# Gating and adding two expert rows on ScalarE and GpSimd, and part of the ALPHA x addition on VectorE

## What is computed

```python
# end of layer 0: combine the experts, post-norm
y = y + dense_gate[:, e:e + 1] * (h @ w_down[e])      # two experts per token have a gate
x = layer_norm(ALPHA * x + f, ln_ffn_g[0], ln_ffn_b[0])
# layer 1: causal pooling over trailing windows 2/4/8/16, one per group of 256 channels
pooled = means - x
mixed = einsum('btgc,gcd->btgd', pooled, w_pool) * pool_scale
x = layer_norm(ALPHA * x + mixed, ln_mix_g[1], ln_mix_b[1])
# then the router of layer 1 reads x
logits = x @ w_router
```

## Time and profile before

| | us |
|---|---|
| median of three runs | 1658.82 (1653.52 to 1663.27) |
| the profiled execution | 1659.36 |
| its span, first to last instruction | 1657.6 |
| mean granted TensorE clock | 0.927 of full |
| busy: TensorE, VectorE, ScalarE, GpSimd | 1457.2, 635.0, 365.4, 205.5 |
| the stage `combine_pool_mix` | about 1134 to 1272 |

### The profile page before, as it was taken

The page is one execution under the profiler, slowest core; times in us unless marked ns, Lnnn a source line. Parts: engine busy times, 40 slices in busy tenths (PEclk is TensorE's granted clock), DMA queues, the critical chain, the costliest instruction groups (busy, mean ns, idle before and its releaser), DMA issues. The chain is left out here.

```text
span 1657.6 us, 27544 instructions
## 1 busy us (share of the span) xinstructions
PE 1457.2 (88%) x10747; PEld 890.2 (54%) x10748; DVE 635.0 (38%) x1062; ACT 365.4 (22%) x788; POOL 205.5 (12%) x263
## 2 busy tenths in 40 slices
PE   6999999957778898999929999994996599999968
PEld 4566666645578886444414444442795344444423
DVE  1122453079245452776461111114795311111127
ACT  1233110066423332111101111111232011111111
POOL 4000000000133322110001101104000110110040
PEclk9999999987789999999959999996697699999989
DMA  6573110041110002110259788785105778786453
GB/s 189 134 290 121 26 26 26 0 113 27 30 26 4 5 4 71 56 39 26 111 169 314 267 303 289 254 282 181 62 1 186 269 246 314 257 281 227 159 209 124
DMA packets 137060, 236.96 MB, mean 143 GB/s; under 512 B 20178, under 2 KB 100115, under 8 KB 136682
## 3 DMA queue, kind: packets, MB, share of 16 engines
q1 hardware_dynamic: 113458, 151.01, 28.7%
q0 software_dynamic: 16880, 60.41, 9.9%
q10 hardware_dynamic: 6624, 24.12, 3.6%
HBM read 178.84 MB, written 58.21 MB: 143 GB/s over the span
## 5 line engine op out<-in xcount | busy, mean ns | idle before, releaser
L2257 PE MATMUL ex_pb<-ew_w_gate_up,ex_xT 128*128 x736 | 329.8, 601 | 6.0 <-DVE ex_xT L2302 2.3
L298 PE MATMUL pj_pb<-pj_xT,pj_w 128*128 128x348 f32 (+3 forms) x960 | 282.1, 455 | 0.8 <-ACT pj_xT L322 0.8
L298 PEld LDWEIGHTS pj_pb<-pj_xT,pj_w 128*128 128x128 f32 (+1 forms) x960 | 178.8, 186 | 101.9 <-ACT pj_xT L322 0.8
L2257 PEld LDWEIGHTS ex_pb<-ew_w_gate_up,ex_xT 128*128 128x128 f32 x736 | 138.0, 193 | 165.0 <-issue 164.0
L2240 PE MATMUL ex_pb<-ew_w_down,ex_hiddenT 128*128 x368 | 165.7, 593 | 3.4 <-ACT ex_hiddenT L2327 3.4
L2450 DVE TENSOR_TENSOR ex_hidden<-ex_hidden,ex_pb 128x256 f32<-128x256 f32 x46 | 19.4, 421 | 324.4 <-ACT ex_hidden L2322 324.4
L2240 PEld LDWEIGHTS ex_pb<-ew_w_down,ex_hiddenT 128*128 128x128 f32 x368 | 66.3, 190 | 69.9 <-issue 69.9
L2445 DVE COPY ex_y_rows<-ex_pb 128x512 f32<-128x512 f32 x46 | 31.8, 692 | 134.5 <-PE ex_pb L2240 134.5
L430 DVE SCALAR_TENSOR_TENSOR mixed<-pj_pb,v_mu,mixed 128x347 f32<-128x347 f32 (+3 forms) x42 | 24.0, 572 | 145.7 <-ACT mixed L372 145.6
L2322 ACT ACTIVATE ex_hidden<-ex_pb 128x256 f32<-128x256 f32 x46 | 17.7, 384 | 261.3 <-PE ex_pb L2257 261.3
L1888 PE MATMUL mo_pb<-late_rows,projected_qkv 128*128 128x512 f32 (+1 forms) x144 | 66.6, 608 | 0.0
(11 more groups left out here) (414 smaller groups left out, 2031.4 us busy)
## 6 DMA issues: line engine op xcount, KB each, us to landing
ew_w_gate_up<-in_w_ex_gate SPq DMA_DIRECT2D x32, 1024.0 KB, 8.2
ew_w_gate_up<-in_w_ex_up SPq DMA_DIRECT2D x32, 1024.0 KB, 10.9
ew_w_down<-in_w_ex_down SPq DMA_DIRECT2D x32, 1024.0 KB, 12.9
scratch_slots_out<-ex_y_rows ACTq DMA_DIRECT2D x46, 512.0 KB, 4.8
scratch_slots_out<-pj_tmp POOLq DMA_DIRECT2D x4, 4096.0 KB, 16.7
scratch_x_stored<-x_rows SPq DMA_DIRECT2D x16, 512.0 KB
pj_w<-in_w_in SPq DMA_DIRECT2D x7, 1024.0 KB, 8.9
minus_kk_then_y<-in_x_prompt SPq DMA_DIRECT2D x8, 512.0 KB, 6.0
```

The source lines that it names most:

```text
L298: last = nc.tensor.matmul(product(at)[:, 0:tn], w[:, s % NW, k, c0:c0 + mrows], xT[:, k, x0:x0 + tn], start=(k == 0), stop=(k == KD - 1))
L2257: last = mm(pb[:, 2 + u, :], xT[:, u, k, :], w[:, k, :], start=(k == 0), stop=(k == KD - 1))
```

## The change

ScalarE multiplies both gathered rows by their gates, in place. GpSimd adds row 1 to row 0, and VectorE adds ALPHA x to that sum in one instruction. GpSimd issues the gathers of the first three tiles, then for each tile the add and the gather of the tile three further on. In the pooling products, TensorE's diagonal adds ALPHA x for the first two groups (columns 0 to 511) only; for the other two VectorE adds ALPHA x to bank 3 in PSUM after the products, ahead of the statistics.

```diff
--- before.py
+++ after.py
@@ -1510,7 +1510,7 @@
         LN = "res st var root rs g x".split()
         qa = {k: m.sem(f"a_{k}") for k in LN}
         qb = {k: m.sem(f"b_{k}") for k in LN}
-        q = {k: m.sem(k) for k in "eps alpha sel first both wscaled band feats tr cp rp rpc rl ev zero keep".split()}
+        q = {k: m.sem(k) for k in "eps alpha sel gated both wscaled band prod feats tr cp rp rpc rl ev zero keep".split()}
         s_r = [m.sem(f"rows{i}") for i in range(TILES)]
         block = m.block()
         steps = range(-1, TILES + 4)
@@ -1534,8 +1534,16 @@
                                             bass.IndirectOffsetOnAxis(ap=slots[0:n, i, c:c + 1], axis=0)).then_inc(s_r[i], 16)
             nc.gpsimd.tensor_scalar(alpha_i[:, :], const["ident"][:, :], ALPHA, None, ALU.mult).then_inc(q["alpha"], 1)
             group_sums(pool, nc.gpsimd, sel, const["ident"], q["sel"])
+            AHEAD = 3
+            for j in range(AHEAD):
+                gather(j)
             for j in range(TILES):
-                gather(j)
+                i = ORDER[j]
+                pool.wait_ge(q["gated"], 2 * j + 2)
+                nc.gpsimd.tensor_tensor(r[0:rows(i), i, 0, :], r[0:rows(i), i, 0, :], r[0:rows(i), i, 1, :], ALU.add)\
+                    .then_inc(q["both"], 1)
+                if j + AHEAD < TILES:
+                    gather(j + AHEAD)
 
         @block.sync
         def _(sp):
@@ -1584,10 +1592,11 @@
                     pe.wait_ge(q["wscaled"], 1)
                 for gi in range(4):
                     at = pb[0:n, 2 + gi // 2, 256 * (gi % 2):256 * (gi % 2) + 256]
-                    mm(at, alpha_i[0:n, 0:n], x_(j)[:, 256 * gi:256 * gi + 256], start=True, stop=False)
+                    if gi < 2:
+                        mm(at, alpha_i[0:n, 0:n], x_(j)[:, 256 * gi:256 * gi + 256], start=True, stop=False)
                     for k in range(2):
-                        last = mm(at, feats[:, j % 2, 2 * gi + k, 0:n], pm.w[:, 2 * gi + k, :], start=False, stop=(k == 1))
-                last.then_inc(qb["res"], 1)
+                        last = mm(at, feats[:, j % 2, 2 * gi + k, 0:n], pm.w[:, 2 * gi + k, :], start=(gi >= 2 and k == 0), stop=(k == 1))
+                last.then_inc(q["prod"], 1)
 
             def transposes(j):
                 i = ORDER[j]
@@ -1635,8 +1644,9 @@
                 i = ORDER[j]
                 n = rows(i)
                 act.wait_ge(s_r[i], 32)
-                nc.scalar.activation(r[0:n, i, 0, :], r[0:n, i, 0, :], ACT.Identity,
-                                     scale=gates[0:n, i, 0:1]).then_inc(q["first"], 1)
+                for c in range(2):
+                    nc.scalar.activation(r[0:n, i, c, :], r[0:n, i, c, :], ACT.Identity,
+                                         scale=gates[0:n, i, c:c + 1]).then_inc(q["gated"], 1)
 
             def copy_x(j):
                 n = rows(ORDER[j])
@@ -1650,7 +1660,7 @@
                 n = rows(ORDER[j])
                 act.wait_ge(q["band"], j + 1)
                 if j >= 2:
-                    act.wait_ge(qb["res"], j - 1)
+                    act.wait_ge(q["prod"], j - 1)
                 nc.scalar.copy(feats[:, j % 2, :, 0:n], pb[:, 0:2, :].rearrange("p b (k t) -> p (b k) t", k=4)[:, :, 0:n])\
                     .then_inc(q["feats"], 1)
             def copy_parts(j):
@@ -1687,11 +1697,14 @@
             def gather_residual(j):
                 i = ORDER[j]
                 n = rows(i)
-                r1, r2 = r[0:n, i, 0, :], r[0:n, i, 1, :]
-                dve.wait_ge(q["first"], j + 1)
-                stt(out=r1, in0=r2, scalar=gates[0:n, i, 1:2], in1=r1, op0=ALU.mult, op1=ALU.add).then_inc(q["both"], 1)
                 dve.wait_ge(q["both"], j + 1)
-                stt(out=x_(j), in0=x_(j), scalar=ALPHA, in1=r1, op0=ALU.mult, op1=ALU.add).then_inc(qa["res"], 1)
+                stt(out=x_(j), in0=x_(j), scalar=ALPHA, in1=r[0:n, i, 0, :], op0=ALU.mult, op1=ALU.add).then_inc(qa["res"], 1)
+
+            def second_residual(j):
+
+                n, half = rows(ORDER[j]), pb[0:rows(ORDER[j]), 3, :]
+                dve.wait_ge(q["prod"], j + 1)
+                stt(out=half, in0=x_(j)[:, 512:1024], scalar=ALPHA, in1=half, op0=ALU.mult, op1=ALU.add).then_inc(qb["res"], 1)
 
             def mixed(j):
                 return pb[0:rows(ORDER[j]), 2:4, :].rearrange("p b n -> p (b n)")
@@ -1702,6 +1715,7 @@
                 nc.vector.tensor_copy(lg[0:rows(i), i, :], pb[0:rows(i), 7, 0:E]).then_inc(q["ev"], 1)
             for s in steps:
                 if live(s - 2):
+                    second_residual(s - 2)
                     norm_stats(nc, dve, qb, s - 2, mixed(s - 2), stb)
                     if s - 2 == 0:
                         dve.wait_ge(q["keep"], 32)
```

## The result

| | before | after |
|---|---|---|
| median | 1658.82 us (17 runs, 1653.52 to 1667.32) | 1672.23 us (17 runs, 1663.96 to 1677.45) |
| ratio, 95% interval | | 1.0076 (1.006 to 1.0093) |
| profiled execution, span | 1657.6 | 1673.9 |
| mean granted clock | 0.927 | 0.915 |

The changed kernel is 13.4 us slower, and 1672 lies just above the range of the prediction (1654 to 1671). The page's first line of the kernel after shows the work moved as the diff says: GpSimd gains 25 us and ScalarE 10 against the earlier trace rows, TensorE and VectorE hardly change.

A forecast was written before the change was run, and what follows sets the result against it. TensorE bounds the whole kernel, but VectorE was taken to set the edited stage's steady tile (10.95 us). Terms +3.1 at the start offset to 0.0, then +5.6 and -0.3, gave +5.3: 1665 us, range 1654 to 1671.

The forecast's parts named there:

- Start: Start of the edited stage: the add waits behind six gather issues, so the first ALPHA x addition comes 3.1 us later.
- The first products: TensorE's products of the sample tile, -1.9 us, and of the next tile, -0.87 at the fast clock.
- R: Start of VectorE's ALPHA x addition (L1694) in a tile; forecast to move 0.0 us after the first products.
- Four tiles: Steady tiles from 1193.43 to 1237.24: GpSimd's add delays finish a by 2.0 us, tile 12.34 us, +5.6 in all.
- rival B: Steady tiles: slow clock delays the gates, the add misses finish b, such tiles take 10.34 us; total 1661, chance 0.20.
- The last two tiles: End of the stage: these tiles run behind TensorE, which saves 0.87 and waits 0.70 each; -0.3 us.
- rival C: Steady tiles: idle time holds TensorE at 1.2 GHz, its tile takes 19.8 us; +35, total 1695, chance 0.05.
- Rival A: Steady tiles: finish a goes first and PSUM work hides the add; four tiles -2.4, sum -2.7, total 1656.7, chance 0.20.

The follow-up runs named there:

- e6: e3 with the sample tile's second gate and add left on VectorE and a fourth tile's gathers issued ahead; 1650.84 us, ratio 0.9965 to the kernel before.
- e4b: The changed kernel with four useless matmuls a tile from the fourth tile on, ahead of TensorE's wait for finish a; 1664.56 us, ratio 1.0045.
- e3: The changed kernel with one more GpSimd wait, so each add starts only after finish a of the tile before; 1656.29 us, ratio 0.9991.
- f1: The changed kernel, unaltered, profiled a second time; profiled execution 1665.99 us, stage 143.09 us.
- e1: The changed kernel with all four TensorE diagonals restored and no PSUM addition, keeping the gates and GpSimd add; 1668.80 us, ratio 1.006.
- e2: The kernel before with only the PSUM half: two diagonals dropped, VectorE adding ALPHA x in PSUM; 1661.94 us, ratio 1.003.

## Why the prediction was wrong, step by step

1. **Start, +3.1.** Right: 13.04 - 9.90 = +3.14, and the same in all three profiles. The cause is right too: with the sample tile back on VectorE (e6) it is gone.
2. and 3. **The first products, R of the fifth tile 0.0 (-0.8 to +0.9).** Measured -1.7, -5.1 and -1.6 us at the fifth addition. The clock rose 51.4 us after the start of the stage before, and 40.8, 33.8 and 41.1 us after it in the three profiles of the change; 13.7, 17.1 and 13.7 us later it fell again for 10.2. I had a clock that rises at the same time as before or 3.4 us later, not one that rises earlier and falls again.
4. **Four tiles, 4 x 1.4 = +5.6.** Measured +6.8, three times over. The pieces were right: the add 2.3 to 2.5 us where it isn't itself held (2.2), the half addition 0.68 to 0.70 (0.70), two gates 2.17 (2.18), the finish held to 3.19 (I had 2.0 us of delay and it is 1.9), and the pure mechanism gives a tile of 12.3 (12.34), as e4b shows in every tile. But the change doesn't do this in every tile. It alternates, as in rival B.
5. **The last two tiles, -0.3.** Measured +3.8, again the same in all three profiles. This is the step that failed most. The last held finish, at 1239.70, is followed by a clock of 0.50 from 1244.2 to 1254.4, and the last tiles, which hang on TensorE, ran through it. In e3 this part is +0.4.

The sum of the stage in the first profile: -1.7 (the start is contained in it, as in the prediction's R) + 6.8 + 3.8 = +8.9, against 0.0 + 5.6 - 0.3 = +5.3. The stage alone would have made 1668, inside the range. The rest of the median's +13.4, some 4.5 us, lies outside of the stage, for which the sum had no term; 3.4 and 3.8 us of it are TensorE's clock behind the stage in two of the three profiles, and its cause is open.

So what failed inside the stage is the clock of 1.00 in steps 4 and 5, and with it **rival B's price**. I saw that 2.4 us of idle time a tile might drop the clock, and that late gates would then let finish a through, and I gave such a tile 10.34 us, VectorE's time. The two such tiles take 13.57 and 12.43 (from 1195.73 and from 1221.58), because VectorE waits for TensorE's products there (3.18 us at 1205.80, 1.96 at 1230.51). The sentence on rival C, that 2.4 us of idle time pay for the first 4.8 us of slow work, was used for C and not for B. The idle time lies in the held tile; the slow work is done in the next, where VectorE waits for it. Had I priced B's tile at TensorE's pace, B would have been slower than the forecast, not faster, and the end of the stage would have had a term of its own.

Rival A's condition isn't met in the changed kernel, but its arithmetic was right: with the add behind finish a (e3) the four tiles are -2.4, as written, and the stage -5.7 against the -2.7 of the sum; the median moved by -2.4, which its interval doesn't tell from none; that it lies so near to -2.7 is partly luck. The one wait of e3 takes away both the collision and the low clock behind it, 16 us together. e3 and e4b both keep the clock at 1.00 in the steady part, and only e4b collides: 11.5 us of the stage (131.94 and 143.44, the latter with the extra matmuls) and 8.3 of the median are the collision's. e4b, which takes away the low clock and keeps the collision, is 7.7 us faster than the change; its stage is 3.0 us shorter than in two of the change's three profiles, and 0.3 longer than in f1, where the clock had risen 7 us earlier than in the other two. How much of the loss is the clock's thus stays between these.

Beyond the size, the chances were badly laid. "Slower by over 0.5%" (8.3 us) had 0.20. With the collision all but certain from the earlier trace rows, a late start that nothing hides, and a steady part whose clock was at 1.00 already, the spread belonged on the slow side.

## What to carry to other kernels

When one engine's work is moved to another, price the moment at which the two meet: an add of 2.3 us was free behind finish a and cost 1.9 us and more in front of it, and one wait moved it. When an engine is relieved in a kernel in which the other sets the pace, its idle time isn't harmless: price the tile after the idle one at TensorE's lower clock. Two edits that each lose (e1, e2) can win together once the meeting is arranged and the start is left alone (e6).

## What the runs showed of the hardware that I had not expected

- The clock can fall inside a stage in which TensorE never waits long. In e2 it was busy 8.56 and 8.55 of 10 us ahead of the fall at 1234.4, with no wait over 1.3 us, and ran at 0.50 for 10.2 us behind it. In e1, at 9.35, it stayed at 1.00, and so it did in e3 behind a window of 8.44 (1178 to 1188). What decides it stays open.
- Useless matmuls in the idle time paid: four a tile took the stage from 146.45 (143.09 and 146.72 in the repeats) to 143.44, and the median from 1672.23 to 1664.56.
- In the collision one of the two is held until the other is through. A finish of 1.28 us takes 3.18 to 3.20 beside the add, in e4b five times of five; where it goes first it keeps its 1.28, and the add takes 3.31 (1227.45 in the change's first profile). Beside a memset it takes 1.28. The half addition with a PSUM operand kept its 0.69 us beside the add in e3.
- An 8-row add takes GpSimd 2.33 us (1149.11), a 128-row one 2.35 (e3): the number of rows made no difference.
